# The order of leading and trailing products inside a feature tile of a split-float32 matmul kernel

## What is computed

```python
# first block
proj = h @ w_in            # 1024 -> 3600, attention + gated delta net on it
x = x + rms_norm(mix @ w_out)
m = square(relu(h @ w_up)) @ w_down         # 1024 -> 4096 -> 1024
x = x + rms_norm(m)
# second block
proj = h @ w_in_2          # 1024 -> 11264: convolution branch, retention, gates
y_a = (gb * conv) @ w_a_out;  y_r = ret @ w_r_out;  x = x + (gated sum) @ w_o
x = x + (silu(h @ w_ff_gate) * (h @ w_ff_up)) @ w_ff_down   # 1024 -> 2816 -> 1024
out = rmsnorm(x, g_final)
```

## Time and profile before

| | |
|---|---|
| median of 3 runs | 912.13 us (911.82 to 912.15) |
| profiled execution, its own time | 912.35 us |
| its span, first to last instruction | 910.5 us |
| PE / PEld busy | 99% / 84% of the span |
| DVE / ACT / POOL busy | 66% / 51% / 10% |
| mean granted TensorE clock | 0.998 |
| memory traffic | 159.8 MB by DMA, 176 GB/s |

### The profile page before, as it was taken

The page is one execution under the profiler, slowest core; times in us unless marked ns, Lnnn a source line. Parts: engine busy times, 40 slices in busy tenths (PEclk is TensorE's granted clock), DMA queues, the critical chain, the costliest instruction groups (busy, mean ns, idle before and its releaser), DMA issues.

```text
span 910.5 us, 12778 instructions
## 1 busy us (share of the span) xinstructions
PE 898.0 (99%) x5466; PEld 765.9 (84%) x5466; DVE 602.7 (66%) x705; ACT 461.4 (51%) x558; POOL 90.9 (10%) x92
## 2 busy tenths in 40 slices
PE   9999999999999999999999999999999999999997
PEld 8989888888888887888888878778788888888886
DVE  6889985777666557687867565555656666564665
ACT  7765554555444446645444255453355555454443
POOL 2142100100000000000125310110100000000000
PEclk9999999999999999999999999999999999999999
DMA  8734523244555554544565534454454356445531
GB/s 325 281 108 177 174 67 117 93 162 185 188 193 198 200 199 179 220 164 161 185 231 185 185 123 188 152 185 166 163 202 163 139 177 236 175 183 223 185 139 47
DMA packets 24218, 159.81 MB, mean 176 GB/s; under 512 B 3241, under 2 KB 3769, under 8 KB 5857
## 3 DMA queue, kind: packets, MB, share of 16 engines
q1 hardware_dynamic: 21600, 152.58, 45.8%
q0 software_dynamic: 2272, 6.24, 2.0%
q10 hardware_dynamic: 288, 0.17, 0.1%
HBM read 157.91 MB, written 2.63 MB: 176 GB/s over the span
## 4 chain that ended last, share of the span: by engine, by line
PE 80%; DVE 12%; ACT 4%; issue 2%; DMA 0%; POOL 0%; POOLq 0%; DVEq 0%; ACTq 0%
PE banks L494 31%; PE banks L462 20%; PE banks L465 10%; DVE t_wl L1582 4%; PE banks L434 4%; PE banks L585 3%; PE banks L522 2%; PE banks L739 2%; PE banks L993 2%; PE banks L405 1%; ACT t_wh L1114 1%; DVE t_hold L1600 1%; DVE t_xt L1600 1%; PE banks L943 1%; PE banks L1075 1%
## 5 line engine op out<-in xcount | busy, mean ns | idle before, releaser
L1582 DVE TENSOR_TENSOR t_wl<-t_raw,t_wh 128x2048 fp32r<-128x2048 f32 x139 | 318.0, 2309 | 123.2 <-ACT t_wh L1114 121.9
L462 PE MATMUL banks<-t_hx,t_wh 128*128 128x512 f32 x992 | 312.0, 396 | 0.0
L1114 ACT CAST t_wh<-t_raw 128x2048 fp32r<-128x2048 f32 x139 | 261.5, 1906 | 12.8 <-DMA t_raw<-in_W 8.1
L465 PEld LDWEIGHTS banks<-t_hx,t_wl 128*128 128x128 f32 x992 | 186.3, 188 | 43.8
L465 PE MATMUL banks<-t_hx,t_wl 128*128 128x256 f32 x992 | 194.9, 278 | 0.0
L462 PEld LDWEIGHTS banks<-t_hx,t_wh 128*128 128x128 f32 x992 | 153.3, 189 | 2.4
L494 PE MATMUL banks<-t_wh,t_hx 128*128 128x512 f32 x320 | 102.3, 396 | 0.0
L494 PEld LDWEIGHTS banks<-t_wh,t_hx 128*128 128x128 f32 x320 | 59.5, 188 | 12.7 <-issue 0.6
L494 PE MATMUL banks<-t_wl,t_hx 128*128 128x512 f32 x160 | 61.1, 390 | 0.0
L434 PE MATMUL banks<-t_hx,t_wh 128*128 128x256 f32 x336 | 60.6, 285 | 0.4 <-ACT t_hx L1157 0.4
L2187 POOL TENSOR_TENSOR t_st<-t_st,t_half 128x1 f32<-128x1 f32 (+1 forms) x18 | 10.6, 589 | 432.5 <-DVE t_st L1608 430.7
(11 more groups left out here) (310 smaller groups left out, 1265.5 us busy)
## 6 DMA issues: line engine op xcount, KB each, us to landing
t_raw<-in_W SPq DMA_DIRECT2D x143, 1024.0 KB, 4.8
skew<-scr POOLq DMA_DIRECT2D x1, 1536.0 KB, 16.3
t_x<-in_x SPq DMA_DIRECT2D x2, 512.0 KB, 4.8
t_tab<-in_tab POOLq DMA_DIRECT2D x1, 640.0 KB, 7.1
out<-t_xt SPq DMA_DIRECT2D x2, 320.0 KB, 2.3
t_raw<-in_W SPq DMA_DIRECT2D x1, 512.0 KB, 6.9
t_T<-skew POOLq DMA_DIRECT2D x4, 128.0 KB, 2.5
t_xt<-skew POOLq DMA_DIRECT2D x4, 128.0 KB, 2.4
```

Of the source, the lines that this page charges most:

```text
L462: e.matmul(bank[b + c], M.wh[:, h, wk], M.hx[:, k, :, :].rearrange("p a s -> p (a s)"), start=k == 0, stop=False)
L465: m = e.matmul(bank[b + c][:, 0:S], M.wl[:, h, wk], M.hh[:, k, :], start=False, stop=k == 7)
L1114: e.copy(M.wh[:, h, 0:n], M.raw[:, r, 0:n]).then_inc(q.sem, q.tick(("hi", i)))
L1582: e.tensor_tensor(M.wl[:, h, 0:n], M.raw[:, r, 0:n], M.wh[:, h, 0:n].bitcast(F32), ALU.subtract).then_inc(q.sem, q.tick(("lo", i)))
```

## The change

In `wide_unit` the two inner loops change places. A step now does tile 0 with leading weights, tile 0 with trailing weights, tile 1 with leading weights, tile 1 with trailing weights. Number, size, operands and banks of the products are the same, and so are the waits before the unit and the signal behind it.

```diff
                 for k in range(8):
                     arrived(k)
-                    for w in range(2):
-                        for c in range(2):
+                    for c in range(2):
+                        for w in range(2):
                             wk = slice(k * 256 + c * 128, k * 256 + c * 128 + 128)
                             if w == 0:
                                 e.matmul(bank[b + c], M.wh[:, h, wk], M.hx[:, k, :, :].rearrange("p a s -> p (a s)"),
```

## The result

The changed kernel takes 916.08 us (median of 4, 915.86 to 916.18) against 912.11 for the kernel before: ratio 1.0044, 95% interval 1.0031 to 1.0056. It is slower by 4.0 us, where 911.5 us and no measurable change was forecast. The profiled execution has a span of 914.1 us against 910.5.

A forecast was written before the change was run, and what follows sets the result against it. PE, busy 99% of the span at full clock, was taken as the bound. All terms were 0 except -1.5 ns per step: over 400 steps -0.6 us, from 912.13 to 911.5 us; range 905.4 to 917.2.

The forecast's parts named there:

- The bound and the place: PE, busy 99% of the span, bounds the kernel; only start-to-start gaps inside the wide unit can move.
- The same bank twice in a row: Wide unit: accumulating a tile's leading and trailing products back to back into one bank costs 0 to 1 ns, taken as 0.
- The price by sizes: Wide-unit step: two products of 512 columns and two of 256 cost 0.6934 us, leaving 3.0 ns of 0.6964 unexplained.
- Loads of the stationary operand: Wide unit: a 0.110 us load just fits behind a 256-column product; both orders have the same covers, so 0.
- What follows a burst of short ones: Wide unit: long products slow after short ones; net 3.0 ns per step could vanish or double, taken as -1.5 ns.
- How much is on the path: Gains count for 400 of 496 wide-unit steps, losses for all 496 less the 0.3 us PE wait near 450 us.
- Rival C: Wide unit: long products stay at 0.2333, short ones cost full 0.120; step 0.7067 us, +4.8 us, 916.9 us; chance 0.25.
- Rival B: Wide unit: single short products cost 0.1133, long ones 0.2267; step 0.680 us, 6.6 us less, 905.6 us; chance 0.29.

The follow-up runs named there:

- e1: Kernel before with the two banks swapped for the trailing products, sizes in the old order: 912.29 us against 912.32, ratio 1.000.
- e2: Changed kernel with each unit's first step in the old order, then sizes alternating and each pair changing bank: 915.61 us, ratio 1.0039 to the kernel before.
- e3: Changed kernel with each unit's first step in the old order, then sizes alternating and each pair in one bank: 915.80 us, ratio 1.0037 to the kernel before.
- e14: Kernel before, old order, with 64 stationary columns instead of 128 in seven of eight k's trailing products: 915.41 us, one run.
- e15: Changed order with 64 stationary columns instead of 128 in seven of eight k's trailing products: 911.82 us, one run.
- e4: Kernel before with all sixteen leading products of a unit first, then all sixteen trailing ones: 912.05 us, ratio 0.9997.
- e10: Changed order with the trailing products at 512 columns instead of 256, so all products have one size: 1015.09 us, one run.

## Why the prediction was wrong

- **The bound and the place** were right. TensorE's gaps inside the wide unit are what moved, the time moved with the step, and the step left the forecast's 0.693 to 0.699.
- **The same bank twice in a row, 0**: right, by e1 and by e2 against e3.
- **The price by sizes, 0.6934 per step**: right as a floor. No steady step of 512 and 256 columns with whole loads fell below it, and no steady step with 320 and 384 columns fell below the price drawn from it. The 3.0 ns left over are 3.2 in the unrounded starts.
- **Loads of the stationary operand, "the sum of covers is unchanged", 0**: the 0.110 us of a load fit (0.108 between the closest starts, 0.113 by the remainder at 192 columns), but the conclusion was wrong. Equal cover did not mean an equal price; there is a price where cover is plentiful (320 and 384 columns), and halving the stationary side of the short products changes it (e14, e15).
- **"What follows a burst of short ones": this is the step that failed.** It took the 3.0 ns as a price per burst or per length, bounded the new order between -3.0 and +3.0, and chose -1.5 because smoother alternation should do slightly better. Measured: +10 ns in the steady slow pattern (0.7067 against 0.6966 unrounded). The surplus over the sizes went from 3 to 13 ns, not from 3 to 0 or 6. The bound was drawn from an average over a pattern, and a pattern's surplus doesn't carry over to another: bursts of four have 8 ns, one burst per unit some 2, half loads 10 in the old order and 0 in the new. That long products need about five in a row until they are back at 0.227 (e4), while the alternation has one at a time, fits a larger surplus, but it does not explain its gaps: the tail has 0.233, 0.236, 0.228, the alternation 0.233, 0.241, 0.236.
- **How much is on the path**: losses were to count in full less 0.3 us. The wait near 450 us did go and gave back about 0.5 us. Right in kind; the gaps ahead of it had a little more slack than the wait showed.
- **Rival C** (chance 0.25) was the case: 0.7067 us per step by its price and 0.7067 measured, 916.9 us against 916.08. That it agrees to the digit is luck, since its two terms were off against each other: long products cost 0.2363 on the mean of the slow pattern, not 0.2333, short ones 0.1170, not 0.120, so "the long ones stay slow" was right, and too little, and "the short ones pay in full" was not. Nor is its place, the gap from a short product to the next long one, where the time goes: that gap is below the short product's 0.120, and the surplus is in the gap of the long product behind it. It also left out the five quick units (0.5 us) and the cheaper first step of many slow ones (0.3 us together); against that stand the 0.4 us of the L494 products.
- **Rival B**, faster than before, shows in a few units only and in a weaker form: 0.6935, no step of 0.680, and with long products at 0.231 and not at its 0.2267. With 192 columns 0.680 appears, but there it is the floor.

What stays open is the mechanism inside TensorE that makes the surplus. The runs exclude the bank (e1, e2 against e3), the clock (granted in full in every run), an operand or tile that costs by itself at equal size (e10), and a load that barely fits as a condition. That an interplay of the stationary side and the moving stream with several steady patterns is behind it is what they leave, and is not shown.

## What to carry to other kernels

Where a stream of matmuls mixes sizes, price it by columns plus a fixed cost per product with the load as a floor, and treat what is left over (here 0 to 27 ns per four products, by the estimates of the table) as belonging to the whole pattern: order, sizes, loads and what stands ahead. In these runs it did not carry over from a neighbouring order, nor from one size to another, not even in sign, so with hundreds of repetitions the order has to be timed. Pairs of equal size, or one block of each, were as good as anything tried at 512 and 256 columns; all leading products first was within 0.1% of pairs.

## What was not expected of the hardware

- One order of instructions has two steady patterns of gaps, 0.6935 and 0.7067 us per four products, and keeps the one into which it enters; with one transpose ahead of the unit 42 of 61 units are in the quick one, against 5.
- With 64 stationary columns in the short products instead of 128 one order became slower by 7 ns and another quicker by 13 ns per step.
- A trailing product of 192 columns cost 0.1133 us in the sum of a step, as much as one of 240 would by the price per column (192 columns would be 0.080 + 0.0133 = 0.0933 us), so 256 columns, at 0.120, cost only 7 ns more than 192.
